# State steps and group norm inside the output units of an attention block, with rounded sums, other banks and a copy moved to ScalarE

## What is computed

```python
# stick-breaking attention, for each block of 128 queries
z = jnp.einsum('bqhd,bkhd->bhqk', qb, kb) * scale
log_fail = jnp.where(strict, jax.nn.log_sigmoid(-z), 0.0)
after = lax.cumsum(log_fail, axis=3, reverse=True) - log_fail
w = jnp.where(strict, jnp.exp(jax.nn.log_sigmoid(z) + after), 0.0)
out = jnp.einsum('bhqk,bkhd->bqhd', w, vb)

# RWKV-7 time mix
kk = kk / jnp.maximum(jnp.linalg.norm(kk, axis=-1, keepdims=True), 1e-12)
y = wkv7_scan(r_h, decay, k_h, v_h, kk, a)         # state over 4 chunks of 64 positions
mean = jnp.mean(y, axis=-1, keepdims=True)
var = jnp.mean(jnp.square(y - mean), axis=-1, keepdims=True)
y = ((y - mean) * lax.rsqrt(var + GN_EPS)) * lnx_w + lnx_b
o_rw = (y + bonus) * g                             # g = sigmoid(xg) @ g_up
merged = gates[..., :D] * (o_sb @ w_sb_out) + gates[..., D:] * (o_rw @ w_rw_out)
```

## Time and profile before

| | us |
|---|---|
| median of 3 runs | 841.4 (840.96 to 841.78) |
| the profiled execution | 841.16 |
| its span, first to last instruction | 839.4 |
| TensorE busy | 824.6 (98%) |
| VectorE busy | 586.9 (70%) |
| ScalarE busy | 430.8 (51%) |
| mean granted TensorE clock | 0.997 |

### The profile page before, as it was taken

How to read it: one execution, slowest core, us unless ns; L and a number is a source line. 1 busy time by engine, 2 the same in 40 slices (tenths; PEclk the granted TensorE clock), 3 DMA queues, 4 the chain that set the end, 5 groups by cost and what they waited for, 6 DMA issues and landing times.

```text
span 839.4 us, 14921 instructions
## 1 busy us (share of the span) xinstructions
PE 824.6 (98%) x6332; PEld 715.2 (85%) x6332; DVE 586.9 (70%) x693; ACT 430.8 (51%) x529; POOL 6.4 (1%) x8
## 2 busy tenths in 40 slices
PE   9999999999999999999998999999999999999997
PEld 9998788888989888888887888888888888888885
DVE  5999865656887666656678567795764866676664
ACT  6644344474387544544466365546654544444443
POOL 0000010000000000000000000000000000000000
PEclk9999999999999999999999999999999999999999
DMA  9845513331764555565545553546423365555541
GB/s 301 289 152 177 175 53 102 103 102 52 280 209 159 180 201 185 165 216 185 200 157 177 168 194 108 192 143 201 167 100 126 133 228 182 180 180 183 192 149 50
DMA packets 96999, 140.55 MB, mean 167 GB/s; under 512 B 2480, under 2 KB 79408, under 8 KB 96944
## 3 DMA queue, kind: packets, MB, share of 16 engines
q1 hardware_dynamic: 96512, 139.36, 49.7%
q10 hardware_dynamic: 432, 0.39, 0.2%
HBM read 138.69 MB, written 1.05 MB: 166 GB/s over the span
## 4 chain that ended last, share of the span: by engine, by line
PE 83%; DVE 10%; ACT 3%; issue 3%; DMA 1%; POOL 0%; ACTq 0%; DVEq 0%; POOLq 0%
PE PS L443 81%; DVE wlo L1762 3%; ACT whi L1271 1%; PE PS L569 1%; DMA raw<-in_w_in_dram 1%; ACT st L1271 1%; DVE rw L1828 1%; ACT xhl L1271 1%; DVE diff L1825 1%; DVE stg L1823 1%; PE PS L1100 0%; DVE cs L1845 0%; PE PS L716 0%; DVE xhl L1789 0%; DVE TT L1924 0%
## 5 line engine op out<-in xcount | busy, mean ns | idle before, releaser
L1762 DVE TENSOR_TENSOR wlo<-raw,whi 128x2048 fp32r<-128x2048 f32 x122 | 278.2, 2289 | 78.7 <-ACT whi L1271 78.5
L443 PE MATMUL PS<-xhl,whi 128*128 128x512 f32 (+1 forms) x1328 | 308.5, 365 | 3.9 <-DVE km L1767 2.9
L1271 ACT ACTIVATE whi<-raw 128x2048 fp32r<-128x2048 f32 (+1 forms) x130 | 241.3, 1859 | 93.6 <-PE PS L443 90.1
L443 PEld LDWEIGHTS PS<-xhl,whi 128*128 128x128 f32 x1328 | 230.3, 190 | 40.3 <-DVE km L1767 3.1
L443 PE MATMUL PS<-xhl,wlo 128*128 128x256 f32 x1136 | 180.3, 282 | 0.1
L443 PEld LDWEIGHTS PS<-xhl,wlo 128*128 128x128 f32 x1136 | 163.7, 191 | 9.7 <-DVE wlo L1803 0.3
L443 PE MATMUL PS<-whi,fh 128*128 128x512 f32 x216 | 84.3, 391 | 0.0
L443 PE MATMUL PS<-wlo,fh 128*128 128x512 f32 x216 | 84.3, 390 | 0.0
L443 PE MATMUL PS<-whi,fl 128*128 128x512 f32 x216 | 84.0, 389 | 0.0
L1767 DVE TENSOR_TENSOR fa<-PS,fa 128x512 f32<-128x512 f32 x25 | 17.3, 691 | 62.7 <-ACT fa L1271 62.7
L443 PEld LDWEIGHTS PS<-whi,fl 128*128 128x128 f32 x216 | 40.6, 188 | 8.6
(11 more groups left out here) (327 smaller groups left out, 1035.3 us busy)
## 6 DMA issues: line engine op xcount, KB each, us to landing
raw<-in_w_in_dram SPq DMA_DIRECT2D x32, 1024.0 KB, 5.3
raw<-in_w_up_dram SPq DMA_DIRECT2D x16, 1024.0 KB, 5.3
raw<-in_w_down_dram SPq DMA_DIRECT2D x16, 1024.0 KB, 5.1
raw<-in_w_ffn_gate_dram SPq DMA_DIRECT2D x11, 1024.0 KB, 5.3
raw<-in_w_ffn_up_dram SPq DMA_DIRECT2D x11, 1024.0 KB, 5.3
raw<-in_w_ffn_down_dram SPq DMA_DIRECT2D x11, 1024.0 KB, 5.6
raw<-in_w_kv_mem_dram SPq DMA_DIRECT2D x8, 1024.0 KB, 5.3
raw<-in_w_o_dram SPq DMA_DIRECT2D x4, 1024.0 KB, 8.2
```

The costliest lines, as they stand in the source:

```text
L443: return nc.tensor.matmul(o, l, r, start=start, stop=stop, **kw)
L1271: return nc.scalar.activation(o, i, f, **kw)
L1762: V.tensor_tensor(wlo[u % RING][:], raw[u % RING][:], whi[u % RING][:].bitcast(f32), ALU.subtract) \
```

## The change

- The sums of the attention take rounded operands: ScalarE copies `st2` into `lfh` (rounded), VectorE writes the rest in place as `lfl`, and TensorE multiplies both with rounded copies of `tri` and `ones`. VectorE's subtraction stands in `gate_unit(2p)`, ahead of the evacuation of the gates.
- ScalarE copies the output gate out of banks 4 and 5 (six copies in all), four of them scaled by `lnx_w`. TensorE waits for `gn_pre`, which is now signalled after the bonus products, and for those copies (`g_read`).
- The four gather products stand at `k` = 0, 2, 4, 6 of the next unit's first column, and the four spread products inside the first unit of `U_QK`, at `k` = 2 and 6 of both columns.
- The state steps from the second on and the group norm stand inside `U_SO[0]` and `U_SO[1]`, with other banks (`Y_BANKS`, `SO_BANKS`). ScalarE rounds the attention's output before the gate sigmoids, and does both `y_out` before the squares.
- VectorE does both `y_center` and both `y_inverse` ahead of its split of `U_RO[0]`.
- The second unit of `U_QK2` goes to banks 2 and 3. Several semaphores are merged (`logits`, `logits_read`, `pair_weights`, `pair_values`), which orders nothing anew.

```diff
+        lfh = at("lfh", W + 88, [P, 2, 384], f32r)
+        lfl = at("lfl", W + 85, [P, 2, 384], f32r)
+        tri_r = at("tri_r", 82.5, [P, P], f32r)
+        ones_r = at("ones_r", 83, [P, P], f32r)
...
-        QK2_BANKS = (None, (0, 1), (6, 7), (0, 1))
+        QK2_BANKS = (None, (2, 3), (6, 7), (0, 1))
+        Y_BANKS = ((4, 5), (4, 7))
+        SO_BANKS = ((6, 1), (2, 3))
...
+            def spread_norms(f, k):
+                if k not in (2, 6):
+                    return
+                j = 2 * f + k // 4
+                if j == 0:
+                    pe.wait_ge(sem("kk_rs"), 1)
+                last = mm(PS[:, 4 * 512 + j * SEQ:4 * 512 + (j + 1) * SEQ], C("spread")[0:NH, j * P:(j + 1) * P], krs[:], True, True)
...
-                by_feature_wide(u, xhl, QK_BANKS[i % 2])
+                by_feature_wide(u, xhl, QK_BANKS[i % 2], amidst=None if i else spread_norms)
...
-                for e in range(2):
-                    mm(PS[:, (4 + e) * 512:(4 + e) * 512 + 384], C("tri"), st2[:, e, :], False, False, skip_group_check=True)
+                for part in (lfh, lfl):
+                    for e in range(2):
+                        mm(PS[:, (4 + e) * 512:(4 + e) * 512 + 384], tri_r[:], part[:, e, :], False, False, skip_group_check=True)
...
+            def steps_second(f, k):
+                if (f, k) == (0, 0):
+                    y_spread(0)
+                if (f, k) == (0, 2):
+                    y_squares(1)
+                if (f, k) == (1, 2):
+                    y_spread(1)
...
-                if i == 1:
+                if i == 2:
+                    pe.wait_ge(sem("out2_evac"), 1)
+                elif i == 3:
                     pe.wait_ge(sem("summed"), halved("km", 2))
...
+            act.wait_ge(sem("bonus_mm"), 1)
+            act.wait_ge(sem("rw_pre"), 1)
+            for j in range(NPAIR):
+                A_(rw[:, j, :], PS[:, 4 * 512 + j * SEQ:4 * 512 + (j + 1) * SEQ], ACT.Copy, scale=par_col("lnx_w", j))
...
+                if i % 2 == 0:
+                    dve.wait_ge(sem("sb_hi"), i // 2 + 1)
+                    dve.wait_ge(sem("sb_masked"), i // 2 + 1)
+                    V.tensor_tensor(lfl[:], st2[:], lfh[:].bitcast(f32), ALU.subtract).then_inc(sem("sb_lf"), 1)
                 g = gates[:, 2 * i:2 * i + 2, :]
...
             y_center(0)
-            tokens_u(3)
+            y_center(1)
             y_inverse(0)
+            y_inverse(1)
             lo(U_G[NH - 1] + RING)
-            y_center(1)
-            y_inverse(1)
             y_scale(0)
             y_scale(1)
```

More of the change, by code:

```diff
@@ L454, in split, with by_feature @@
                         wlo[u % RING][:].rearrange("p (k n) -> p k n", n=n))
-            def by_feature(u, hi, lo, b, st=None, between=None, later=0, amidst=None):
+            def by_feature(u, hi, lo, b, st=None, between=None, later=0, amidst=None, banks=None):
                 n = units[u][1]
@@ L506, in by_feature @@
                 for f in range(n // P):
-                    o = PS[:, b * 512 + f * SEQ:b * 512 + (f + 1) * SEQ]
+                    o = bank(banks[f // 2] if banks else b + f // 2)[:, f % 2 * SEQ:(f % 2 + 1) * SEQ]
                     for k in range(kt):
@@ L662, in _ @@
                     pe.wait_ge(sem("out_evac"), i - 2)
[L663 to L672 removed]
+                by_feature(u, xh, xl, RW_BANK[i], None if i else "n1", amid_first(i), 0, gather_squares if i == 5 else None)
             for i, u in enumerate(U_QK):
@@ L1021, in _, with steps_first @@
-            by_feature(U_SO[1], sboh, sbol, 2)
+            state_values(1)
+            def steps_first(f, k):
+                if (f, k) == (0, 2):
+                    state_rest(1)
+                    y_state(1)
+                    y_rest(0)
+                    y_rest(1)
+                    state_part(2)
+                    state_values(2)
+                if (f, k) == (1, 0):
+                    state_rest(2)
+                    pe.wait_ge(sem("y_evac"), 1)
+                    y_values(1)
+                    y_state(2)
+                    y_rest(2)
+                    state_part(3)
+                if (f, k) == (1, 2):
+                    y_state(3)
+                    pe.wait_ge(sem("u_ready"), 3)
+                    y_rest(3)
+                    y_sum(0)
+                if (f, k) == (2, 0):
+                    y_sum(1)
+                if (f, k) == (3, 0):
+                    y_squares(0)
@@ L1090, in dilated_logits @@
                     last = mm(PS[:, (4 + e) * 512 + P:(4 + e) * 512 + 384], q2[half(e), p_, P:SEQ], k2[half(e), p_, :], True, True)
-                last.then_inc(sem("d_z"), 1)
+                last.then_inc(sem("logits"), 1)
             def dilated_turn(p_):
@@ L1394, in _ @@
             A_(eX[:], sg[:], ACT.Exp, scale=-c0).then_inc(sem("decays"), 1)
+            act.wait_ge(sem("cst_loaded"), 16)
+            A_(tri_r[:], C("tri"), ACT.Copy)
+            A_(ones_r[:], C("ones"), ACT.Copy)
             for i, u in enumerate(U_QK):
@@ L1399, in _ @@
             hi(U_V[0] + RING)
+            act.wait_ge(sem("bonus_mm"), 1)
+            act.wait_ge(sem("rw_pre"), 1)
+            for j in range(NPAIR):
+                A_(rw[:, j, :], PS[:, 4 * 512 + j * SEQ:4 * 512 + (j + 1) * SEQ], ACT.Copy, scale=par_col("lnx_w", j))
+            for j in range(2):
+                last = A_(rw[:, 4 + 2 * j:6 + 2 * j, :], bank(4 + j).rearrange("p (j t) -> p j t", j=2), ACT.Copy)
+            last.then_inc(sem("g_read"), 1)
             after(U_V[1])
@@ L1894, in _ @@
             dve.wait_ge(sem("bonus_mm"), 1)
-            dve.wait_ge(sem("rw_pre"), 1)
-            for j in range(NPAIR):
-                V.tensor_scalar(rw[:, j, :], PS[:, 4 * 512 + j * SEQ:4 * 512 + (j + 1) * SEQ], par_col("lnx_w", j), None, ALU.mult)
             for j in range(2):
@@ L2054, in gate @@
                     g = gates[:, base + 4 * i + 2 * c:base + 4 * i + 2 * c + 2, :].rearrange("p f t -> p (f t)")
-                    last = V.tensor_tensor(g, bank(2 * i + c), g, ALU.mult)
+                    last = V.tensor_tensor(g, bank(SO_BANKS[i][c] if base == 0 else 2 * i + c), g, ALU.mult)
                 return last
```

162 lines of the change are left out of this document (72 added, 90 removed).

## The result

| | before | changed |
|---|---|---|
| median of the runs, us | 841.25 (839.58 to 841.78, 8 runs) | 847.35 (845.19 to 850.96, 8 runs) |
| ratio, 95% interval | | 1.0079 [1.0064, 1.0094] |
| span of the profiled execution, us | 839.4 | 849.2 |
| mean granted TensorE clock, all runs | | 0.986 to 0.995 |

What follows compares the result with a forecast made beforehand. TensorE, busy 98% of the span, was taken as the bound. Terms 3.0 + 0 + 0.7 - 1.7 + 4.0 - 4.7 = +1.3 us on 841.4 gave 842.7 us; its own range 840.5 to 844.5, with rivals 838.7 to 847.0.

Steps and rivals of the forecast that it cites:

- the price of the krs spread, +3.0: First U_QK unit: new wait on krs and three more trips, less old waits regained; net +3.0 us (1.8 to 3.7).
- the old wait before the logits: TensorE's wait before the first logits in the kernel before; its removal was forecast to give back 1.9 us.
- The fall of the clock: Rival, chance 0.27: clock halves after new waits before U_RO and in U_QK; 844.4 us for the first, 846 for both.
- Its price of 1.6 to 1.7: Clock rival's cost before U_RO: 3.4 us at 1.2 GHz give back half, +1.6 to 1.7 us.
- the row of 1.9 us without a fall: Trace of the kernel before: after 1.9 us without a product, before the first logits, TensorE ran at full clock.
- The output gate, 0: ScalarE's copies before the first logits: 0 us more, same wait already gone; without TensorE's later arrival, -1.9.
- Rounded sums, +0.7 and -1.7: Attention sums: pair 0 loses 0.7 us (0 to 1.2), pairs 1 to 3 gain 1.7 (0.6 to 2.4).
- the estimate of 2.6: Sums of three pairs: gain of 2.6 us by the four-pass rule for float32; the forecast kept 1.7 instead.
- State steps, +4.0: State steps inside output units: new wait of 3.7 us before U_RO, +4.0 us (2.5 to 5.0).
- The banks of U_QK2, -4.7: Second U_QK2 unit: wait and half clock after it vanish, -4.7 us (-4.2 to -4.9).
- The rival that the bank change was not what it says: Rival, chance 0.11: second U_QK2 unit waits for something as late as km, 4.7 us come back, 847.4 us.
- the +1.3 forecast: Whole kernel: sum of all forecast terms, +1.3 us, giving 842.7 us.

Runs made afterwards that it cites:

- e5: Changed kernel with VectorE's maximum and reciprocal of krs moved ahead of its split of the weights in the same turn: 842.03 us, ratio 1.0006.
- e2: Changed kernel with VectorE's split of the first U_RO unit put between the two reciprocals of the group norm: 846.3 us, ratio 1.0054.
- e14: The changed kernel, unchanged, run and profiled once more: 847.01 us, ratio 1.0085.
- e11: Changed kernel with the four krs spread products four 512-column products later in the same unit: 845.72 us, ratio 1.0054.
- e10: Changed kernel with VectorE's maximum and reciprocal of krs moved 3 us later, behind the eight operations of k_mod: 852.62 us, ratio 1.0137.
- e13: Changed kernel with the four krs products grouped behind the first U_QK unit, TensorE still waiting for krs after its second product: 843.70 us, ratio 1.0022.
- e4: Kernel before with only the banks of the second U_QK2 unit and the waits that go with them changed: 836.84 us, ratio 0.9948.
- e9: Kernel before with only the banks of U_QK2 and the output gate's copies by ScalarE: 836.02 us, ratio 0.9934.
- e12: Kernel before plus ScalarE's output gate, U_QK2 banks and rounded sums for pairs 1 to 3 only, pair 0 in float32: 833.03 us, ratio 0.9903.
- e8: Changed kernel with krs and kq groups, state steps and group norm as before, leaving ScalarE's output gate, rounded sums and U_QK2 banks: 833.58 us, ratio 0.9899.
- e3: Changed kernel with the wait on krs kept in place, but all four spread products there in one group: 846.39 us, ratio 1.0070.

## Why the prediction was wrong, point by point

**The step that failed is the price of the krs spread, +3.0: it put nothing for the clock.** Its mechanism was there: a wait where it was forecast (2.7 us from 54.9 to 57.6, forecast 3.0 from 54.5 to 57.5), ended by the reciprocal, and 1.3 us for three trips, forecast 1.2. Without a fall of the clock the term would have been right within a us. TensorE's order in `e5` is the same and its clock stays up; the first `krs,cst` comes there 15.45 us after `kq,cst`, in the changed kernel 17.65. So the stage without a fall is 55.0 + 2.2 = 57.2 us against 54.7 before, **+2.5**, with the old wait before the logits and the `kq` trips counted. What the term left out is the clock. The same stage took 58.7 in `e2`, 60.3 in `e14` and 64.6 in the first profile, with 3.4, 6.8 and 17.1 us of half clock: falls cost **1.5, 3.1 and 7.4 us**. For the medians: the fastest runs of `e11`, with a wait 0.9 shorter, took 842.84, and the fastest of `e5`, with one 2.2 shorter, 841.5, so the changed kernel with its clock up at `krs` would take an estimated 843.7. None of its thirteen runs is below 845.19 or has a mean clock above 0.995. Its median fall thus costs 847.35 - 843.7 = 3.6 us, an estimate, and the term is +6.1 in the median and +9.9 in the profiled run (64.6 - 54.7).

**The fall of the clock was a rival, and came at both waits.** I gave it 0.27 with the argument that one fall in the trace is one case; all runs of the changed kernel had it, by their times. Its price of 1.6 to 1.7 was nearly right before `U_RO`: from there to `whi,mh` 12.9 to 13.1 us in six profiles with 3.4 us of half clock, against 11.52, so 1.4 to 1.6; with 6.8 us of it (`e10`, `e11`) 13.9 and 14.2, so 2.4 and 2.7. At `krs` it was the price of a fall like that of the earlier trace rows, and this was too small: 3.4 us at half clock in one profile of a kernel with this wait, 17.1 in another. That is how the time came to 847.35, above the 846 that this rival gave for both places. I also read the row of 1.9 us without a fall as a bound; with 1.8 us and the four products behind it the clock fell in `e11`. The Trainium skill (TensorE: Matmul & The Clock Gate, HAM oscillation) says that idle stretches between bursts throttle the clock again and again. The runs agree for the waits of 2.7 us and more, though with 2.7 us of wait alone (`e13`) in five of ten runs only; a fall should have been the likeliest case and not the second.

**The output gate, 0.** Right as a sum, by another account: ScalarE's copies alone give 1.8 us (`e4` and `e9`: 10.81 and 9.00 in the stage), as the text said they would without a later TensorE.

**Rounded sums, +0.7 and -1.7.** Pair 0 lost 0.35, inside the bounds and half of what was taken, by the wait on `Tm` that was named; `e12` takes it back. Pairs 1 to 3 gained 1.76 (68.36 to 66.60), 0.59 each. The Trainium skill (FP8 and Floating Point Precision, TensorE Precision Notes) says that a true float32 product takes four passes; the estimate of 2.6 worked out from it is not borne out. It is not the float32 group that is off: pair 2's took 1.76 us (from 150.72 to the next product at 152.48) for the 1.7 by that rule. The rounded group took 1.20 (160.62 to 161.82), not 0.85.

**State steps, +4.0.** Measured +4.4 (28.68 to 33.11), with a wait of 3.6 us for the 3.7 forecast. VectorE's split behind the second reciprocal is late, and `e2` shows it: VectorE had been idle for 3.64 us before. Then +1.4 for the clock. `e2` and `e8` show both parts: the split's place is worth 3.4 with the clock, the old order 2.2 more. In the changed kernel VectorE's 1.28 us of `gates` also stand between its last step on `yc` and the last `rwol`; to move them was not tried.

**The banks of U_QK2, -4.7.** Measured -4.67 (557.97 to 553.30) and 4.6 alone in `e4`. The rival that the bank change was not what it says fell.

**The sum.** With measured sizes and without the two falls, the parts give 2.5 + 0.35 - 1.76 + 4.4 - 4.67 = +0.8 for the +1.3 forecast. In the profiled executions the falls add 7.4 + 1.4, +9.6 in all, and 0.2 stand ahead of `kq,cst`: that is the whole 9.8 between the spans of 839.4 and 849.2. In the medians they add some 3.6 + 1.5, +5.9, beside the 6.1 measured. That the sum without the falls came so near is partly luck: the forecast had the krs term 0.5 and pair 0's loss 0.35 too high, and the state steps 0.4 too low.

**What stays open.** The runs don't settle what decides whether the clock falls and for how long. The wait's length doesn't order it in the profiled runs. At `krs`:

| profiled run | wait, us | the four products | half clock, us |
|---|---|---|---|
| `e5` | 0.5 | scattered behind it | none |
| `e11` | 1.8 | scattered behind it, closer | 63.3 to 66.8 |
| `e13` | 2.7 | none near it | 58.2 to 61.6 |
| `e2` | 2.7 | scattered behind it | 60.4 to 63.8 |
| `e3` | 2.7 | in one group behind it | 59.1 to 65.9 |
| `e14` | 2.7 | scattered behind it | 57.7 to 64.5 |
| changed | 2.7 | scattered behind it | 57.1 to 74.2 |
| `e10` | 5.6 | scattered behind it | 58.5 to 68.7 |

The float32 products of `krs`, which have 8 rows, seem to have a part in it: the wait of 2.7 us with them had a fall in all runs, the same wait alone in half, and in `e9` the clock fell behind them with no wait at all. That is argued from these cases and not shown: a kernel with the wait and rounded products in their place was not tried.

## What to carry to other kernels

A wait put in front of a busy TensorE is not a cost of its length alone: in this kernel, with waits of 1.8 to 5.6 us, a fall of the clock came with it in most runs. It cost 1.4 to 2.7 us before `U_RO` and some 3.6 in the median at `krs`. Before a product is moved ahead, move its producer ahead too: `e5` and `e2`, each a few lines on VectorE, took away much of what the two moves had cost (5.3 us of the median at `krs`; 3.4 in the stages before `U_RO`). And take large changes apart: three parts of this one, without pair 0's sums, gain 8.3 us on the kernel before (`e12`), hidden under two that lose more.
